# Two attention stages rewritten: stick-breaking attention with queries on the partitions, latent attention in fp32r parts

## The reference, cut to what matters

```
z = einsum('bqhd,bkhd->bhqk', q, k) * 64 ** -0.5
before = key_pos[None, :] < q_pos[:, None]
log_not = where(before, log_sigmoid(-z), 0.0)
suffix = cumsum(log_not, axis=3, reverse=True) - log_not
w = where(before, exp(log_sigmoid(z) + suffix), 0.0)
out = einsum('bhqk,bkhd->bqhd', w, v)
```

```
scores = (einsum(q_nope, k_nope[:e]) + einsum(q_rope, k_rope[:e])) * 192 ** -0.5
probs = softmax(where(s + arange(128)[:, None] >= arange(e)[None, :], scores, -inf))
out = einsum('bhqk,bkhd->bqhd', probs, v[:, :e])
```

## Time and profile before

| what | value |
|---|---|
| median of 3 runs | 5151.81 us (5148.06 to 5152.1) |
| the profiled execution's own time | 5159.39 us |
| its span, first to last instruction | 5157.6 us |
| busy share of the span: PE, PEld, DVE, ACT, POOL | 80%, 61%, 54%, 38%, 14% |
| mean granted TensorE clock | 0.887 |
| stick stage, first DMA issue to the next phase's | 418.1 to 721.3 us: 303.2 us |
| latent stage, likewise | 4251.6 to 4413.9 us: 162.3 us |

### The profile page before, as it was taken

How to read it: one execution, slowest core, us unless ns; L and a number is a source line. 1 busy time by engine, 2 the same in 40 slices (tenths; PEclk the granted TensorE clock), 3 DMA queues, 4 the chain that set the end, 5 groups by cost and what they waited for, 6 DMA issues and landing times. The chain is left out here.

```text
span 5157.6 us, 53350 instructions
## 1 busy us (share of the span) xinstructions
PE 4143.9 (80%) x18650; PEld 3137.2 (61%) x18650; DVE 2770.8 (54%) x3247; ACT 1946.1 (38%) x2595; POOL 717.6 (14%) x582
## 2 busy tenths in 40 slices
PE   7997966959995895978759999999969947333679
PEld 5874434427883773844648888888848826222667
DVE  3126756132113777634269999999962233457332
ACT  2115643031112663221227777777731123310123
POOL 1003433014000222002100000101013000013000
PEclk8998988979997997989869999999979969755789
DMA  3321122422222004142149999999933232354351
GB/s 96 98 81 49 31 73 62 163 70 90 95 95 95 19 15 141 57 172 94 59 180 402 384 391 385 386 383 383 384 101 98 83 114 72 133 170 104 76 138 53
DMA packets 485166, 783.37 MB, mean 152 GB/s; under 512 B 172079, under 2 KB 309551, under 8 KB 483880
## 3 DMA queue, kind: packets, MB, share of 16 engines
q1 hardware_dynamic: 449224, 682.55, 37.8%
q10 hardware_dynamic: 31200, 82.32, 4.3%
q0 software_dynamic: 4608, 16.78, 1.2%
HBM read 657.43 MB, written 120.59 MB: 151 GB/s over the span
## 5 line engine op out<-in xcount | busy, mean ns | idle before, releaser
L71 PE MATMUL b_in_acc<-b_in_acts_hi,b_in_w_hi 128*128 128x512 f32 (+1 forms) x1456 | 579.4, 398 | 51.3 <-POOL b_in_acts_lo L749 21.9
L72 PE MATMUL b_in_acc<-b_in_acts_lo,b_in_w_hi 128*128 128x512 f32 (+1 forms) x1456 | 572.7, 393 | 0.0
L73 PE MATMUL b_in_acc<-b_in_acts_hi,b_in_w_lo 128*128 128x512 f32 (+1 forms) x1456 | 572.6, 393 | 0.0
L3140 DVE TENSOR_TENSOR experts_w_lo<-top_xT,experts_w_hi 128x2048 fp32r<-128x2048 f32 x192 | 437.4, 2290 | 60.6 <-ACT experts_w_hi L3085 60.6
L3140 DVE TENSOR_TENSOR experts_w_lo<-experts_ring,experts_w_hi 128x2048 fp32r<-128x2048 f32 x192 | 435.9, 2288 | 33.1 <-ACT experts_w_hi L3085 31.0
L66 DVE CAST b_in_w_hi<-b_in_w 128x1024 fp32r<-128x1024 f32 (+1 forms) x91 | 68.0, 750 | 701.9 <-PE b_in_acc L73 701.9
L3085 ACT ACTIVATE experts_w_hi<-top_xT 128x2048 fp32r<-128x2048 f32 x192 | 367.8, 1919 | 127.8 <-PE experts_gate L73 72.5
L559 ACT ACTIVATE b_in_out<-b_in_acc 128x512 f32<-128x512 f32 (+1 forms) x182 | 109.0, 599 | 809.8 <-PE b_in_acc L73 807.8
L3085 ACT ACTIVATE experts_w_hi<-experts_ring 128x2048 fp32r<-128x2048 f32 x192 | 367.8, 1921 | 115.3 <-PE experts_up L73 64.3
L71 PEld LDWEIGHTS b_in_acc<-b_in_acts_hi,b_in_w_hi 128*128 128x128 f32 (+1 forms) x1456 | 275.2, 189 | 131.8 <-POOL b_in_acts_lo L749 35.9
L73 PEld LDWEIGHTS b_in_acc<-b_in_acts_hi,b_in_w_lo 128*128 128x128 f32 (+1 forms) x1456 | 276.1, 190 | 59.4
(11 more groups left out here) (642 smaller groups left out, 9066.8 us busy)
## 6 DMA issues: line engine op xcount, KB each, us to landing
experts_ring<-in_w_gate SPq DMA_DIRECT2D x128, 1024.0 KB, 7.7
top_xT<-in_w_up SPq DMA_DIRECT2D x128, 1024.0 KB, 10.1
experts_ring<-in_w_down SPq DMA_DIRECT2D x64, 1024.0 KB, 9.9
top_xT<-in_w_down SPq DMA_DIRECT2D x64, 1024.0 KB, 9.6
b_in_w<-in_w_in SPq DMA_DIRECT2D x90, 512.0 KB, 3.9
proj<-b_in_out ACTq DMA_DIRECT2D x90, 512.0 KB, 2.7
mod_w<-in_w_mod SPq DMA_DIRECT2D x12, 2048.0 KB
merge_gate<-proj SPq DMA_DIRECT2D x24, 512.0 KB, 6.1
```

What stands on the lines that cost most here:

```text
L71: nc.tensor.matmul(out, w_hi, x_hi, start=start, stop=False)
L72: nc.tensor.matmul(out, w_hi, x_lo, start=False, stop=False)
L73: return nc.tensor.matmul(out, w_lo, x_hi, start=False, stop=stop)
L3140: nc.vector.tensor_tensor(w_lo[n % HIS][:, :, :], ring[n % RING], w_hi[n % HIS][:, :, :].bitcast(F32), ALU.subtract).then_inc(lo_ready, 1)
```

## The change

Both phases are replaced, and the loops are written out. No other phase changes.

**Stick stage.** Queries now lie on the partitions. A unit is one head and one tile of 128 queries, 64 units in all, unit i of a head against its first i + 1 key tiles in pieces of up to 512 columns. q and k of a head are loaded twice, into both halves of the partitions. ScalarE makes high parts and VectorE low parts; `q_two` holds the high part of q above the low part, so each piece is two fp32r products (with the high and the low part of k), and a mask product on the diagonal tile. ScalarE takes two sigmoids of each piece, of -z (`stay`) and of z (`take`). VectorE multiplies up the `stay` values from the last key to the first in one scan along the free axis, and multiplies `take` by it. TensorE transposes the weights, ScalarE copies them out of PSUM, and one fp32 product for each key tile serves two query tiles side by side. GpSimd has no work left.

**Latent stage.** Scores are five fp32r products in place of two fp32 ones (q_hi k_hi, q_hi k_lo, q_lo k_hi, and the rotated part, high above low, with two parts of the rotated key), and the mask. The scale goes into the split of k. Negation goes into the maximum, the division moves from ScalarE to VectorE, the copy of the transposed probabilities from VectorE to ScalarE, and products serve pairs of query tiles. There are four buffers for the probabilities and two PSUM tiles for the transposes.

In both, a head's split is placed two or three units into the head before it, and results are stored by SP.

The diff, cut to its core:

```diff
-def attend_phase(nc, name, ident, n_heads, parts, v_src, out_dram, out_row0, dv, nk, scale, causal_mask=None):
...
+def latent_attend_phase(nc, name, ident, causal, n_heads, q_rows, qr_rows, k_rows, kr_rows, v_rows, out_rows, scale):
+    NQ = T // P
+    NU = n_heads * NQ
+    PROBS, STATS, AHEAD = 4, 4, 2
+    SPLIT_AT = 2
...
+            def score(j):
+                hd, i = units[j]
+                b, nk = hd % 2, (i + 1) * P
+                if i == 0:
+                    pe.wait_ge(split_done, 3 * hd + 3)
+                if j >= 2:
+                    pe.wait_ge(exp_ready, j - 1)
+                t = slice(i * P, nk)
+                for k0 in range(0, nk, HALF):
+                    k = slice(k0, min(k0 + HALF, nk))
+                    out = score_ps[j % 2][:, k]
+                    nc.tensor.matmul(out, q_hi[b][:, t], k_hi[b][:, k], start=True, stop=False, skip_group_check=True)
+                    nc.tensor.matmul(out, q_hi[b][:, t], k_lo[b][:, k], start=False, stop=False, skip_group_check=True)
+                    nc.tensor.matmul(out, q_lo[b][:, t], k_hi[b][:, k], start=False, stop=False, skip_group_check=True)
+                    nc.tensor.matmul(out, r_two[b][:, t], kr_hi[:, k], start=False, stop=False, skip_group_check=True)
+                    nc.tensor.matmul(out, r_two[b][:, t], kr_lo[:, k], start=False, stop=True, skip_group_check=True)
+                nc.tensor.matmul(score_ps[j % 2][:, t], eye[:, :], mask[:, :], start=False, stop=True,
+                                 skip_group_check=True).then_inc(scored, 1)
...
+            def product(m):
+                hd, i = units[2 * m]
+                pe.wait_ge(turned_copied, turned_through(2 * m + 1))
+                if m >= 2:
+                    pe.wait_ge(o_copied, m - 1)
+                for b in range(i + 2):
+                    n0 = P if b == i + 1 else 0
+                    mm = nc.tensor.matmul(o_ps[m % 2][:, n0:], v_sb[hd % 2][:, b, :], pT[m % 2][:, b, n0:], start=(b == 0),
+                                          stop=(b == i + 1), skip_group_check=True)
+                mm.then_inc(o_ready, 1)
...
+            for j in range(AHEAD):
+                score(j)
+            x = 2
+            for j in range(NU):
+                if j + AHEAD < NU:
+                    score(j + AHEAD)
+                while x < len(turns) and (turns[x][0] == "v" or turns[x][1] <= j):
+                    turn(x)
+                    x += 1
+                if j >= 3 and j % 2 == 1:
+                    product((j - 3) // 2)
+            product(NU // 2 - 1)
...
+            def exponent(j):
+                i, s = units[j][1], j % STATS
+                nk = (i + 1) * P
+                act.wait_ge(top_ready, j + 1)
+                if j >= PROBS:
+                    act.wait_ge(turned_ready, turned_through(j - PROBS))
+                nc.scalar.activation(probs[j % PROBS][:, 0:nk], score_ps[j % 2][:, 0:nk], ACT.Exp, bias=neg_top[:, s:s + 1],
+                                     accum_out=total[:, s:s + 1]).then_inc(exp_ready, 1)
...
+            split(0)
+            copy_turned(0)
+            copy_turned(1)
+            exponent(0)
+            split(1)
...
+            def maximum(j):
+                nk, s = (units[j][1] + 1) * P, j % STATS
+                dve.wait_ge(scored, j + 1)
+                nc.vector.reduce_max(neg_top[:, s:s + 1], score_ps[j % 2][:, 0:nk], AX.X, negate=True).then_inc(top_ready, 1)
+
+            def divide(j):
+                nk, s = (units[j][1] + 1) * P, j % STATS
+                dve.wait_ge(exp_ready, j + 1)
+                nc.vector.reciprocal(inv[:, s:s + 1], total[:, s:s + 1]).then_inc(inv_ready, 1)
+                dve.wait_ge(inv_ready, j + 1)
+                p = probs[j % PROBS][:, 0:nk]
+                nc.vector.tensor_scalar(p, p, inv[:, s:s + 1], None, ALU.mult).then_inc(probs_ready, 1)
...
+            def copy_out(m):
+                dve.wait_ge(o_ready, m + 1)
+                if m >= 2:
+                    dve.wait_ge(stored[m % 2], 16 * (m // 2))
+                nc.vector.tensor_copy(out_sb[m % 2][:, :], o_ps[m % 2][:, :]).then_inc(o_copied, 1)
...
+            maximum(0)
+            split(1)
+            for j in range(NU):
+                if j + 1 < NU:
+                    maximum(j + 1)
+                divide(j)
+                if units[j][1] == SPLIT_AT and 1 <= units[j][0] < n_heads - 1:
+                    split(units[j][0] + 1)
+                if j >= 5 and j % 2 == 1:
+                    copy_out((j - 5) // 2)
...
-def stick_phase(nc, name, ident, strict, neg_future, neg_upper, neg_ones, qT, kT, vT, out_rows, n_heads):
...
+def stick_phase(nc, name, ident, neg_future, qT, kT, vT, out_rows, n_heads):
+
+
+
+
+
+
+    NQ = T // P
+    NU, PAIRS = n_heads * NQ, n_heads // 2
+    RING, SIG, STAY, POST = 4, 4, 3, 2
+    SPLIT_AT = 3
...
+            def score(j):
+                hd, i = units[j]
+                b = hd % 2
+                if i == 0:
+                    pe.wait_ge(split_done, 2 * hd + 2)
+                q = q_two[b][:, i * P:(i + 1) * P]
+                for x in range(pieces_to[j], pieces_to[j + 1]):
+                    _, k0, kn = pieces[x]
+                    out = piece_ps[x % RING]
+                    last = k0 + kn == (i + 1) * P
+                    if x >= RING:
+                        pe.wait_ge(take_ready, x - RING + 1)
+                    nc.tensor.matmul(out[:, 0:kn], q, k_hi[b][:, k0:k0 + kn], start=True, stop=False, skip_group_check=True)
+                    mm = nc.tensor.matmul(out[:, 0:kn], q, k_lo[b][:, k0:k0 + kn], start=False, stop=True, skip_group_check=True)
+                    if last:
+                        mm = nc.tensor.matmul(out[:, kn - P:kn], mask[:, :], eye[:, :], start=False, stop=True, skip_group_check=True)
+                    mm.then_inc(piece_ready, 1)
...
+            for j in range(3):
+                score(j)
+            x = 2
+            for j in range(NU):
+                if j + 3 < NU:
+                    score(j + 3)
+                while x < len(turns) and (turns[x][0] == "v" or turns[x][1] <= j):
+                    turn(x)
+                    x += 1
+                if j >= 3 and j % 2 == 1:
+                    product((j - 3) // 2)
...
+            def sigmoids(j):
+                if j >= STAY:
+                    act.wait_ge(later_ready, j - STAY + 1)
+                if j >= SIG:
+                    act.wait_ge(turned_ready, turned_through(j - SIG))
+                for sign, out, ready in ((-1.0, stay[j % STAY], stay_ready), (1.0, take[j % SIG], take_ready)):
+                    for x in range(pieces_to[j], pieces_to[j + 1]):
+                        _, k0, kn = pieces[x]
+                        if sign < 0:
+                            act.wait_ge(piece_ready, x + 1)
+                        nc.scalar.activation(out[:, k0:k0 + kn], piece_ps[x % RING][:, 0:kn], ACT.Sigmoid,
+                                             scale=sign * 64 ** -0.5).then_inc(ready, 1)
...
+            split(0)
+            copy_turned(0)
+            copy_turned(1)
+            split(1)
+            sigmoids(0)
+            sigmoids(1)
+            x = 2
+            for j in range(NU):
+                if j + 2 < NU:
+                    sigmoids(j + 2)
+                if units[j][1] == SPLIT_AT and 1 <= units[j][0] < n_heads - 1:
+                    split(units[j][0] + 1)
+                while x < len(turns) and (turns[x][0] == "v" or turns[x][1] <= j):
+                    copy_turned(x)
...
+            for j, (hd, i) in enumerate(units):
+                b, nk = j % SIG, (i + 1) * P
+                dve.wait_ge(stay_ready, pieces_to[j + 1])
+                after = later[j % POST]
+                first = T - nk
+                nc.vector.tensor_tensor_scan(out=after[:, T - 1:(first - 1 if first else None):-1], data0=stay[j % STAY][:, nk - 1::-1],
+                                             data1=ones[:, 0:nk], initial=1.0, op0=ALU.mult, op1=ALU.mult).then_inc(later_ready, 1)
+                dve.wait_ge(take_ready, pieces_to[j + 1])
+                dve.wait_ge(later_ready, j + 1)
+                nc.vector.tensor_tensor(take[b][:, 0:nk], take[b][:, 0:nk], after[:, first + 1:T + 1], ALU.mult).then_inc(weights_ready, 1)
+                if i == SPLIT_AT and 1 <= hd < n_heads - 1:
+                    split(hd + 1)
+                if j >= 5 and j % 2 == 1:
+                    copy_out((j - 5) // 2)
```

More of the change, by code:

```diff
@@ new lines, in _ @@
+            pe.wait_ge(consts_ready, 2)
+            turn(0)
+            turn(1)
+            pe.wait_ge(kr_ready, 1)
+            for j in range(AHEAD):
[9 more added lines that the diff above has]
+                    product((j - 3) // 2)
@@ new lines, in turn @@
+            def turn(x):
+                kind, a, g = turns[x]
+                if x >= 2:
+                    pe.wait_ge(turned_copied, x - 1)
+                if kind == "v":
```

(21 more changed lines are left out.)

594 lines of the change are left out of this document (231 added, 363 removed).

## The result

The changed kernel takes 5057.99 us (median of 4 runs, 5054.9 to 5061.72), the kernel before 5151.95 in the same session: a ratio of 0.9817, 95% interval 0.9800 to 0.9834, or 94 us saved. The forecast was 5018 (134 saved), its range 4985 to 5075. The profiled execution took 5060.78 us, with a span of 5059.0 and a mean granted clock of 0.880 (0.887 before).

What follows compares the result with a forecast made beforehand. Before, each stage was a loop over engines, the heaviest three quarters busy; afterwards VectorE bounds stick, TensorE latent. Savings of 98 + 36 = 134 us off 5159.4 give 5025, or 5018 us by the median; range 4985 to 5075.

Steps and rivals of the forecast that it cites:

- rival (1): Both stages: engines wait for each other as in the grouped attention, 79% use, saved 73 + 20, 5059 us; chance 0.22.
- Work of each engine: Busy time summed per engine; stick stage: VectorE 168 us, ScalarE 162, TensorE 139; latent: TensorE 97.5, VectorE 75, ScalarE 71.
- Start of the stick stage: From first load issue to first scan: copies of v, second head's split, table load, a sigmoid; 14.2 us.
- about 1.2 us a head: Stick stage, where a new head begins: ScalarE's split behind TensorE's products makes VectorE's split late; 8 us in all.
- at the other places I find slack: Stick stage away from head starts: PSUM pieces, `take` and `stay` buffers leave about two units (4 to 6 us) of room.
- Steady part: Stick stage after the first scan: VectorE's 163 us plus 10 for hand-overs and 8 at head starts; 181 us.
- hand-overs: Stick stage, between engines: 0.15 us a unit, 10 us in all.
- The tail: End of the stick stage: transposes 0.9, copies 1.2, last product 3.2, output 0.4; 5.7 us.
- Rival (3): TensorE's clock falls: 5205 us at the low level throughout; VectorE hides up to a third in stick stage; chance 0.05.
- gaps of two us: Rival (3)'s condition in the stick stage: TensorE idle a quarter of the time, with such gaps in units 4 to 7.
- Rival (4): Split's extra loads, 8 MB of q and k instead of 4, are issued a head ahead and cost nothing; no chance given.
- The latent stage: TensorE bounds it: start 19.7 us, left on TensorE 94, stalls 7, chain's end 2, hand-over 3.3; 126 us, saved 36.

Runs made afterwards that it cites:

- Three edits of order: Changed kernel with ScalarE's split one unit earlier, all paired products ahead of transposes, VectorE's half behind unit 4: stick stage 203.6 us, ratio 0.9751 to the kernel before.
- the fill: Changed kernel plus 40 TensorE transposes of a constant in the idle gap before unit 4's transposes, in six heads: stick stage 242.2 us.

## Why the prediction was right or wrong

**The total** was right only as a range: 94 us saved, 134 forecast. It landed on rival (1)'s time, but not by its mechanism. The stick stage missed by 41 us: 1.9 at the start, 34.4 in the steady part, 4.7 in the tail. Three edits of order gave all of it back (203.6 us against the 205 forecast), and the program's ratio then is 0.975, where the forecast's 5018 us are 0.974.

**Work of each engine: right, ScalarE's too dear.** VectorE 163 us (168 forecast, with the scan as priced), latent ScalarE 65 (71) and VectorE 65 (75). ScalarE in the stick stage is 137 us, not 162: I added whole durations, and back to back its instructions overlap (two sigmoid pieces of 512 and 128 columns take 0.80 us, not 0.60 + 0.27; all durations add up to 171). VectorE's durations add up to 169, so its term was right and 5 us of it overlap too. ScalarE wasn't the bound, so nothing followed.

**Start of the stick stage:** first scan at 434.8, 16.1 us in, where 14.2 were forecast.

**The step that failed: "about 1.2 us a head", where a new head begins.** I had seen the products of units 6 and 7 ahead of unit 2's transposes and named the late split, but put ScalarE's half ahead of the copy of unit 2. It stands behind it and behind the sigmoids of unit 5, and a second product (units 4 and 5, 2.6 us) is in front too. VectorE waits 5.6 us for it in each of six heads, and moving ScalarE's half gave 24 to 27 us back, over 4 a head, where 1.2 was forecast. Scans of 1024 columns start 29.4 us apart on average from head 0 to head 6 (181 / 8 = 22.6 forecast, 24.8 with ScalarE's split moved). Next to it stood "at the other places I find slack", wrong by 15 us of waits for outputs: the same products, queued behind transposes that themselves wait for VectorE. Steady part: 215.4 us measured from the first scan to the end of VectorE's last unit, 181 forecast; the two rows of waits are 48.7 us, where all stalls together had 18. (VectorE is busy for 156 us of it, all its listed waits are 53 us, and gaps too short to be listed 7, against the 10 forecast for hand-overs.)

**The tail:** 10.4 us where 5.7 were forecast. With the product of units 4 and 5 moved ahead and the clock up (1.00), the shortest stage has a tail of 5.9 us (612.97 to 618.82), so its own terms add up rightly. What it left out are the 12 records queued in front of the last product, 2.6 us, and by difference 2 us of low clock (0.67 from 650 to 660 us).

**Rival (1), waits for each other,** gave the right sum out of wrong terms: it saved 73 and 20 us, measured are 57 and 34. And it is not the cause: with the same buffers and the same instructions the stage reaches 203.6 us. If it shows at all, it is in the last few us, where an edit moves a wait and leaves the head's length.

**Rival (3), the clock,** was there, 0.50 for some 6 us a head, and was priced by the fill: at most 4 us. Its condition "gaps of two us" was too mild (5.3), but its argument that VectorE hides up to a third of low clock is borne out: a mean of 0.83 is what a third of the stage at 0.50 and the rest at 1.00 give. **Rival (4)**, the extra loads, cost nothing visible: no wait for a load stands in the steady part.

**The latent stage:** 128.1 us for 126, with two misses that partly cancel. The first transposes of probabilities came 25.4 us in (19.7 forecast; ScalarE and VectorE waited for the loads of both heads), and behind them TensorE needed 94.2 us to its last products and 5.8 for those, 100 where 94 + 7 + 2 were forecast. That the total is within 2 us of the forecast is partly luck.

## What to carry to other kernels

When an operation that recurs once a head is split over two engines, write out each queue's order around it and follow the chain through all of them, also through what stands ahead of the thing it waits behind; a split that "comes late" was nearly five times dearer than guessed, and either half may be moved to mend it. Put work that is ready ahead of work that must wait for the leading engine, on each engine, but look whom it delays. And a low clock behind a gap may be no more than a sign of the gap, as here: fill it once with idle work to see what the clock itself costs, before blaming it.

## What the runs showed of the hardware

VectorE's instructions with two SBUF operands and GpSimd's didn't run side by side here: 0.96 us became 3.00 and 2.01 became 3.83 in each of six heads, while a copy from PSUM in the same place kept its 0.41. Work moved from VectorE to an idle GpSimd cost VectorE more time (23 us) than it had taken there (14.7 us). Instructions of ScalarE that follow each other at once overlap: 171 us of durations are 137 us of busy time in the stick stage.
